# Two transformer blocks on one core: slots of the weight ring dealt by expected release, and two seams whose first weight tiles feed two units from four channel blocks

## What is computed

```
h = x + concat(mla(a), swa(a)) @ w_out            # a = rms_norm(x) ; a @ w_in feeds both attentions
h = h + square(relu(rms_norm(h) @ w_up)) @ w_down # first MLP, hidden width 8192
x = rms_norm(h)
mod = silu(c) @ w_ada + b_ada                     # 6 x 2048 values: shift, scale, gate (1 and 2)
z = (x * (1 + sc1) + sh1) @ w_in_2 + b_in_2       # 9216 wide: gating branch, hyena branch, gates
y_a = spatial_gating(...) @ w_branch_a ; y_b = hyena(...) @ w_branch_b
x = layer_norm(ALPHA * x + g1 * ((gate_a * y_a + gate_b * y_b) @ w_o + b_o))
h = x * (1 + sc2) + sh2
x = layer_norm(ALPHA * x + g2 * (square(relu(h @ w_m1 + b_m1)) @ w_m2 + b_m2))
```

## Time and profile before

| | |
|---|---|
| median of 3 runs | 2429.3 us (2428.83 to 2429.86) |
| profiled execution | 2428.58 us, of which the span in the trace is 2426.8 us |
| PE busy | 2376.5 us, 98% of the span |
| DVE, ACT busy | 1710.0 us (70%), 1049.4 us (43%) |
| loads of the stream | 498 of 1 MB, median 4.9 us from issue to landing |
| granted PE clock | 0.996 of full speed over the span |

### The profile page before, as it was taken

One profiled execution on the slowest core, in us unless ns is written; L12 is line 12 of the kernel. 1 busy time (PEld: TensorE's weight loads), 2 busy tenths in 40 slices (PEclk: granted clock), 3 DMA queues, 4 the chain that ended last, 5 costly groups with the idle time before them and its releaser, 6 DMA issues.

```text
span 2426.8 us, 30941 instructions
## 1 busy us (share of the span) xinstructions
PE 2376.5 (98%) x13376; PEld 2051.0 (85%) x13376; DVE 1710.0 (70%) x1559; ACT 1049.4 (43%) x999; POOL 29.8 (1%) x61
## 2 busy tenths in 40 slices
PE   7999999999999999989999999999999999999998
PEld 7998888888778888878888888997888888888887
DVE  7777577878777777765677666787764566774665
ACT  5464544434334334455645443343543443443443
POOL 0000000000000000000000000000000000000000
PEclk9999999999999999999999999999999999999999
DMA  7334477777777787775545547875455557775553
GB/s 274 134 130 151 174 262 287 288 290 271 280 294 278 296 309 285 299 268 189 211 162 181 184 177 269 299 278 200 173 190 197 186 190 301 273 278 211 186 193 110
DMA packets 79816, 558.73 MB, mean 230 GB/s; under 512 B 9034, under 2 KB 11285, under 8 KB 13248
## 3 DMA queue, kind: packets, MB, share of 16 engines
q1 hardware_dynamic: 74832, 528.25, 58.9%
q0 software_dynamic: 4848, 28.50, 3.3%
HBM read 547.26 MB, written 9.45 MB: 229 GB/s over the span
## 4 chain that ended last, share of the span: by engine, by line
PE 90%; DVE 4%; DMA 3%; ACT 2%; issue 1%; SPq 0%; ACTq 0%; DVEq 0%
PE ps L582 27%; PE ps L585 13%; PE ps L613 12%; PE ps L615 12%; PE ps L614 12%; DMA stage<-wstream 3%; PE ps L550 2%; PE ps L551 2%; PE ps L552 2%; DVE w_lo L1509 2%; ACT w_hi L1055 1%; PE ps L580 1%; PE ps L625 1%; PE ps L627 1%; PE ps L626 1%
## 5 line engine op out<-in xcount | busy, mean ns | idle before, releaser
L1509 DVE TENSOR_TENSOR w_lo<-stage,w_hi 128x2048 fp32r<-128x2048 f32 x402 | 918.4, 2288 | 459.0 <-ACT w_hi L1055 455.1
L1055 ACT ACTIVATE w_hi<-stage 128x2048 fp32r<-128x2048 f32 x402 | 766.6, 1911 | 755.1 <-DMA stage<-wstream 402.8
L582 PE MATMUL ps<-xs,w_hi 128*128 128x512 f32 x3200 | 998.5, 397 | 16.1 <-DVE w_lo L1509 14.0
L585 PEld LDWEIGHTS ps<-xs,w_lo 128*128 128x128 f32 x3000 | 564.9, 188 | 132.0
L585 PE MATMUL ps<-xs,w_lo 128*128 128x256 f32 x3000 | 591.6, 279 | 0.0
L582 PEld LDWEIGHTS ps<-xs,w_hi 128*128 128x128 f32 x3200 | 495.7, 189 | 31.2 <-DVE w_lo L1509 17.6
L613 PE MATMUL ps<-w_hi,hs 128*128 128x512 f32 x1008 | 394.4, 391 | 0.0
L615 PE MATMUL ps<-w_lo,hs 128*128 128x512 f32 x1008 | 392.7, 390 | 0.0
L614 PE MATMUL ps<-w_hi,hs 128*128 128x512 f32 x1008 | 392.6, 389 | 0.0
L613 PEld LDWEIGHTS ps<-w_hi,hs 128*128 128x128 f32 x1008 | 189.3, 188 | 41.7 <-issue 2.2
L614 PEld LDWEIGHTS ps<-w_hi,hs 128*128 128x128 f32 x1008 | 189.3, 188 | 39.7 <-issue 0.7
(11 more groups left out here) (414 smaller groups left out, 2248.2 us busy)
## 6 DMA issues: line engine op xcount, KB each, us to landing
stage<-wstream SPq DMA_DIRECT2D x497, 1024.0 KB, 4.9
spectra<-k_made POOLq DMA_DIRECT2D x4, 1024.0 KB, 7.7
k_spec<-spectra POOLq DMA_DIRECT2D x4, 1024.0 KB, 6.4
xraw<-xT SPq DMA_DIRECT2D x4, 512.0 KB, 11.4
resid<-x SPq DMA_DIRECT2D x2, 1024.0 KB, 15.7
w<-w POOLq DMA_DIRECT2D x16, 128.0 KB, 5.9
parked<-resid POOLq DMA_DIRECT2D x1, 2048.0 KB, 7.4
resid<-parked POOLq DMA_DIRECT2D x1, 2048.0 KB, 9.0
```

Source lines behind the costliest of these rows:

```text
L582: mm = pe.matmul(out[c], hi[c], rhs[:, k, :], start=(first and j == 0), stop=end)
L585: mm = pe.matmul(out[c][:, S:2 * S], lo[c], rhs[:, k, 0:S], start=False, stop=False)
L1055: act.activation(w_hi[:, w % HIGH, 0:m], stage[:, n % RING, 0:m], ACT.Copy).then_inc(hi_ready, 1)
L1509: tt(w_lo[:, slot, 0:m], stage[:, slot, 0:m], f(w_hi[:, w % HIGH, 0:m]), ALU.subtract).then_inc(lo_ready, 1)
```

## The change

**Slots.** `slots()` deals the five slots by an expected release time in units of tiles: a weight tile k frees its slot at k + 1.0, a chunk behind tile k at k - 1.1. Each load takes the slot that is expected free first and waits for what held it (`HELD_BY`). `ORDER` itself is as before, and so are `RING` and `HIGH`.

**Two-unit tiles.** Tiles 170 and 171 (and 274 and 275) are laid out anew ("quad"): each holds four of the 128-channel blocks (512 channels) of both units 80 and 81. Tile 170 needs block 0 alone, tile 171 block 1 alone. Tiles 172 and 173 hold the upper eight channel blocks of unit 80 and of unit 81, as before. The number of matmuls is the same.

**The seams' order.** PE turns two blocks before tile 170, block 2 in the middle of tile 170 and block 3 in the middle of tile 171. Of block 0 the first two of its four parts get a semaphore of their own (`first_turned`), so that DVE may begin after 4 of 8 transposes. ACT's scaling of block 3 stands behind its work on block 1. Tile 171 (275) is split at step 169 (273), which had no split; the waits of tile 171 for `seam_lower` and `seam_upper` are gone.

```diff
 WHERE = {what: n for n, what in enumerate(ORDER)}
+def slots():
+    free, uses = [-1.0 + i / RING for i in range(RING)], [0] * RING
+    held, k = [None] * RING, 0
+    slot, use, held_by = [], [], []
+    for n, (kind, i) in enumerate(ORDER):
+        k = i if kind == "w" else k
+        s = min(range(RING), key=lambda j: free[j])
+        uses[s] += 1
+        slot.append(s)
+        use.append(uses[s])
+        held_by.append(held[s])
+        held[s] = n
+        free[s] = k + 1.0 if kind == "w" else k - 1.1
+    return slot, use, held_by
+SLOT, USE, HELD_BY = slots()
 def place(w):
...
         return "tok", U_WOUT + n + (4 if kq >= 2 else 0), 4 * kq
+    if w in (T_Z, T_Z + 1):
+        return "quad", U_Z, 4 * (w - T_Z)
+    if w in (T_MLP2, T_MLP2 + 1):
+        return "quad", U_MLP2, 4 * (w - T_MLP2)
     if T_Z <= w < T_BA:
...
-    TURN = (4, 6, 2, 4)
+    TURN = (4, 6, 4, 6)
...
             m = columns_of(ORDER[n][1]) if ORDER[n][0] == "w" else TILE
-            sp.dma_start(stage[:, n % RING, 0:m], ws[n][:, 0:m]).then_inc(loaded[n % RING], 16)
+            sp.dma_start(stage[:, SLOT[n], 0:m], ws[n][:, 0:m]).then_inc(loaded[SLOT[n]], 16)
...
         load(4)
         for n in range(RING, len(ORDER)):
-            kind, k = ORDER[n - RING]
+            kind, k = ORDER[HELD_BY[n]]
             if kind == "w":
                 sp.wait_ge(tile_done, k + 1)
...
+        def two_units(w, rhs, k0, u, first, ready, hook):
+            for j in range(4):
+                k = k0 + j
+                if j == 2:
+                    hook()
+                if j % 2 == 0:
+                    pe.wait_ge(*ready(k // 2))
+                for v in range(2):
+                    out = [ps[:, 2 * ((u + v) % 2) + c, :] for c in range(2)]
+                    a = [1024 * v + (j * 2 + c) * P for c in range(2)]
+                    for c in range(2):
+                        pe.matmul(out[c], w_hi[:, w % HIGH, a[c]:a[c] + P], rhs[:, k, :], start=(first and j == 0),
+                                  stop=False)
+                    for c in range(2):
+                        mm = pe.matmul(out[c][:, S:2 * S], w_lo[:, SLOT[place(w)], a[c]:a[c] + P], rhs[:, k, 0:S],
+                                       start=False, stop=False)
+            return mm
         def tokens_apart(w, rhs, k0, u):
...
                 mm = weights_moved(w, rhs, 0, 4, u + 1, 1024, True, True, ready)
+            elif kind == "quad":
+                if first:
+                    pe.wait_ge(psum_free[(u + 1) % 2], (u + 1) // 2)
+                mm = two_units(w, rhs, k0, u, first, ready, hook)
             elif kind == "tok":
...
                 q, l = divmod(w - t0, QT)
                 if l < UPT:
-                    if t0 == T_MLP2 and w == t0 + 1:
-                        pe.wait_ge(sem("seam_lower"), since("ln1", "lower") + 3)
-                        pe.wait_ge(sem("seam_upper"), since("ln1", "upper") + 3)
-                    tile(w, xs, rhs_ready if w < t0 + 4 else None, hook if w == t0 else None)
+                    turn = (lambda: hook(2 + w - t0)) if hook is not None and w < t0 + 2 else None
+                    tile(w, xs, rhs_ready if w < t0 + 4 else None, turn)
                     if after is not None and w == t0:
                         after()
...
             elif n:
                 pe.wait_ge(sem("seam_scaled"), since(name, "scaled") + n)
-            if n == 3:
-                pe.wait_ge(sem("seam_lo"), since(name, "lo") + 2)
-            turn_block(n, TURN[n], (sem("seam_normed"), since(name, "normed")) if n == 0 else None).then_inc(sem("seam_turned"), 1)
+            if n >= 2:
+                pe.wait_ge(sem("seam_lo"), since(name, "lo") + n)
+            if n == 0:
+                for half in range(2):
+                    for t in range(NB):
+                        pe.wait_ge(sem("seam_normed"), since(name, "normed") + t + 1)
+                        for c in range(2):
+                            a = P * (2 * half + c)
+                            mm = pe.transpose(ps[:, TURN[0] + half, c * S + t * P:c * S + t * P + P],
+                                              resid[:, t, a:a + P], ident[:])
+                    mm.then_inc(sem("seam_turned" if half else "first_turned"), 1)
+                return
+            turn_block(n, TURN[n]).then_inc(sem("seam_turned"), 1)
...
-                pe.wait_ge(sem("seam_upper"), since("f", "upper") + 3)
             tile(w, xs, (lambda h: (sem("seam_lo"), since("f", "lo") + (h + 1 if h < 2 else h // 2 + 2))) if w < T_Z + 4 else None,
-                 (lambda: turn_normed("f", 3)) if w == T_Z else None)
+                 (lambda: turn_normed("f", 2 + w - T_Z)) if w < T_Z + 2 else None)
             if w in (T_Z + 10, T_Z + 14):
...
             turn_normed("ln1", n)
-        mlp(T_MLP2, U_MLP2, lambda h: (sem("seam_lo"), since("ln1", "lo") + (h + 1 if h < 2 else h // 2 + 2)), hook=lambda: turn_normed("ln1", 3))
+        mlp(T_MLP2, U_MLP2, lambda h: (sem("seam_lo"), since("ln1", "lo") + (h + 1 if h < 2 else h // 2 + 2)), hook=lambda n: turn_normed("ln1", n))
         pe.wait_ge(evac_done, U_END)
         for n in range(4):
             if n == 1:
...
             n = place(w)
-            act.wait_ge(loaded[n % RING], 16 * (n // RING + 1))
+            act.wait_ge(loaded[SLOT[n]], 16 * USE[n])
             if w >= HIGH:
                 act.wait_ge(tile_done, w - HIGH + 1)
             m = columns_of(w)
...
             act.activation(root_[:], var[:], ACT.Sqrt).then_inc(sem("token_root_ready"), 1)
-        def normed_hi(name, n, sh, sc, w):
+        def first_hi(name, sh, sc):
+            act.wait_ge(sem("seam_lower"), since(name, "lower") + 1)
+            act.activation(xs[:, 0:2, 0:S], turned[:, 0, 0:2], ACT.Copy).then_inc(sem("seam_hi"), 1)
+            act.wait_ge(sem("seam_turned"), since(name, "turned") + 1)
+            src = turned_bank(TURN[0])
+            for k in (2, 3):
+                ins = act.activation(turned[:, 0, k], src[:, k, :], ACT.Identity, bias=mod[:, sh + k:sh + k + 1],
+                                     scale=mod[:, sc + k:sc + k + 1])
+            ins.then_inc(sem("seam_upper"), 1)
+            act.wait_ge(sem("seam_upper"), since(name, "upper") + 1)
+            act.activation(xs[:, 2:4, 0:S], turned[:, 0, 2:4], ACT.Copy).then_inc(sem("seam_hi"), 1)
+        def normed_hi(name, n, sh, sc):
...
-                act.wait_ge(sem("seam_lower"), since(name, "lower") + 1)
-                act.activation(xs[:, 0:2, 0:S], turned[:, 0, 0:2], ACT.Copy).then_inc(sem("seam_hi"), 1)
-                act.wait_ge(sem("seam_upper"), since(name, "upper") + 1)
-                act.activation(xs[:, 2:4, 0:S], turned[:, 0, 2:4], ACT.Copy).then_inc(sem("seam_hi"), 1)
-                return
-            if n == 2:
-                split(w)
             act.wait_ge(sem("seam_upper"), since(name, "upper") + n + 1)
...
-        def into_stage(name, sh, sc, w):
+        def into_stage(name, sh, sc):
             act.wait_ge(sem("seam_scaled"), since(name, "scaled") + 1)
             scale_block(name, 2)
-            normed_hi(name, 0, sh, sc, w)
+            first_hi(name, sh, sc)
+            normed_hi(name, 1, sh, sc)
             scale_block(name, 3)
-            for n in range(1, 4):
-                normed_hi(name, n, sh, sc, w)
+            for n in range(2, 4):
+                normed_hi(name, n, sh, sc)
         act.wait_ge(sem("ones_ready"), 1)
...
-            if w not in LAST:
-                split(w + 2)
+            split(w + 2)
             if w == T_MLP1:
...
         for w in range(T_WO, T_MLP2):
-            if w not in LAST:
-                split(w + 2)
+            split(w + 2)
             if w == T_WO:
                 mix_hi(U_WO - 1)
...
-            dve.wait_ge(sem("seam_turned"), since(name, "turned") + n + 1)
+            if n:
+                dve.wait_ge(sem("seam_turned"), since(name, "turned") + n + 1)
+            else:
+                dve.wait_ge(sem("first_turned"), ("f", "ln1").index(name) + 1)
...
-        def into_stage(name, sh, sc, w):
+        def into_stage(name, sh, sc):
             normed(name, 0)
             normed(name, 1)
...
             normed_lower(name, 2, sh, sc)
-            split(w)
             normed_lo(name, 2)
...
         for w in range(T_WO, T_MLP2):
-            if w not in LAST:
-                split(w + 2)
-                condition(w + 2)
...
+def by_quarters(t):
+    both = [np.concatenate([t[0][:, a:a + TILE // 2], t[2][:, a:a + TILE // 2]], axis=1) for a in (0, TILE // 2)]
+    return np.concatenate([np.stack(both), t[[1, 3]], t[4:]])
```

More of the change, by code:

```diff
@@ L548, in weights_moved @@
                     o2 = acc(u)[:, c]
-                    hi, lo = w_hi[:, w % HIGH, a:a + P], w_lo[:, place(w) % RING, a:a + P]
+                    hi, lo = w_hi[:, w % HIGH, a:a + P], w_lo[:, SLOT[place(w)], a:a + P]
                     pe.matmul(o2, hi, rhs[:, k, 0:S], start=(first and j == 0), stop=False)
@@ L559, in narrow @@
```

(34 more changed lines are left out.)

9 lines of the change are left out of this document (2 added, 7 removed).

## The result

| | before | changed |
|---|---|---|
| median | 2429.4 us (4 runs, 2428.8 to 2429.9) | 2462.3 us (4 runs, 2460.8 to 2464.1) |
| profiled execution, its span | 2428.58, 2426.8 us | 2460.79, 2459.0 us |
| PE busy | 2376.5 us | 2388.2 us |

The ratio is 1.0136, with a 95% interval of 1.0118 to 1.0154: 33 us slower, where I had forecast 11 and a range that ended at 2449. The direction was right and the size was not.

A forecast was written before the change was run, and what follows sets the result against it. PE, busy 98% of the span, was taken as the bound. Loop 5.3, seams 0.6 and 2.0, clock 3.4 gave +11.3 us on 2428.58, 2439.9; the median 0.7 higher, 2440.6 us; range 2421 to 2449.

The forecast's parts named there:

- The loop: First MLP: load, high part, remainder, sum, next load take 11.28 us per two tiles, slower than PE; net +5.3 us.
- The start: Loop begins at tile 106's end, 702.09 us; the sum of a34 is ready 6.5 us later, at 708.6.
- The steps: From a34 to a69, 23 steps of 11.28 us and 12 of 7.1 us, 344.6 us in all.
- The credit: Second quarter of the first MLP: earlier loads remove its waits and give back 2.6 us.
- The bound above: Upper limit of the first MLP's term: +11 us, with hand-over delays at two pairs and loads 0.1 us longer.
- The load's duration: 1 MB load alone in the queue takes the row's 4.78 us, not the skill's estimated 4.4 us.
- Seam "f": Between tiles 169 and 172: first matmul 0.85 us earlier, but tile 172 starts +0.6 us late after a 3.6 us wait.
- Seam "ln1": Between tiles 273 and 276: tile 275's split delays the first token half 1.15 us; tile 276 starts +2.0 us late.
- The clock at the seams: Two new 3.6 us waits, each followed by 3.4 us at half clock: +3.4 us, bounds 0 and 6.8.
- Chunks a70 to a95: After seam "f": 11.28 us against PE's 11.17, 2.9 us behind at the end, less than the 5.6 us lead.
- A: Rival: slots work and the loop has room; first MLP gives 13 us, seams cost 2.6 to 6.0; chance 0.25.

The follow-up runs named there:

- k + 0.4: The changed kernel with a chunk's slot expected free at k + 0.4 in place of k - 1.1: 2423.4 us, ratio 0.9968.
- k - 0.6: The changed kernel with a chunk's slot expected free at k - 0.6 in place of k - 1.1: 2419.9 us, ratio 0.9954.
- The slots alone: The kernel before, its seams untouched, with the new table of slots: 2455.1 us, ratio 1.0096.
- the shorter sums: The changed kernel with DVE summing only 1024 or 1792 of each chunk's 2048 columns: 2420.8 us and 2444.9 us.
- the seams alone: The changed kernel with load n in slot n % 5 as before: 2439.3 us, ratio 1.0032.

## Why the prediction was right in direction and wrong in size

**The loop: right mechanism, its term mis-sized, 24.4 us and not 5.3.** The step that failed is this term: the loop's start, its count of slow steps and the 2.6 us given back. The forecast put the sum of a34 at 708.6 and that of a69 at 1053.2; the rest to the end of tile 169, 15.5 us, was right (15.7). Three parts make the 19 us:

- *The start, 5.8 us.* I let the loop begin at the end of tile 106, with everything ahead of it loaded, and put 6.5 us from there to the sum of a34. It was running already. The chain of waits of the changed kernel at that place:

```profile
695.91 4.85 DMA stage<-wstream
...
700.78 2.31 DVE stage L1875 x2
...
703.11 4.82 DMA stage<-wstream
...
707.95 1.93 ACT w_hi L1107
...
709.90 2.29 DVE w_lo L1565
712.19 2.22 DVE stage L1875 x2
...
714.42 6.95 DMA stage<-wstream
```

  The load of w109, which I had issued at 702.09 by tile 106's end, was held by the sum of a33 and issued at 703.11. That is only 1.0 us. The other 4.8 us are my 6.5: no row shows such a step, and from the issue of w109 to the sum of a34 it is a full turn of the loop, 11.3 us, as it was from w119's load on the earlier trace rows. The loop was in place long before: every load that waits for a chunk was issued within 0.03 us of that chunk's sum (in the kernel before 4 us or more behind it), and from a1 to a7 the steps are 11.3 to 11.4 us already. 17 chunks in 32 tiles are one in 1.9 tiles, nearly as dense as the third quarter's 19. The forecast said that they are rare there; its own count in the description of the stages said otherwise.
- *The steps, 10.5 us.* The 35 steps took 1069.5 - 714.4 = 355.1 us in place of 344.6. The ordinary step (11.3) and the short one (7.1 to 7.3) were right. But four of the twelve short ones took 8.34 us, and two of the others 12.91 and 13.45; these six are 8.8 of the 10.5 us. DVE in order of time shows one of the former, a43's sum (line 1875) at 806.27:

```profile
800.87 0.69 DVE L1890 SCALAR_TENSOR_TENSOR tev<-tev 128x512 f32<-128x512 f32 x1
802.26 0.69 DVE L1892 TENSOR_TENSOR hs<-tev,hs 128x512 fp32r<-128x512 f32 x1 [0.70 <-ACT hs L1348]
804.06 2.29 DVE L1565 TENSOR_TENSOR w_lo<-stage,w_hi 128x2048 fp32r<-128x2048 f32 x1 [1.11 <-ACT w_hi L1107]
806.27 2.28 DVE L1875 SCALAR_TENSOR_TENSOR stage<-stage,cond 128x2048 f32<-128x2048 f32 x1
```

  The unit's hand-over holds the next split on ACT, and the chunk's sum, which stands behind that split in DVE's order, starts only then; its load had landed at 805.14. The forecast had this as a bound, "about 1.3 us at a pair, two pairs"; it was 1.2 us at four. Of the long steps one is the same hand-over ahead of a56's sum. The other ends the chain above: w111's load took 6.95 us; the load before it in the queue, issued at 704.92, had not landed yet when it was issued, but at 717.84.
- *The credit, 2.6 us.* The end of the loop was a time on the clock, so the waits of the second quarter couldn't be taken off it once more. By the trace they didn't go either: 3.6 us of waits lie from 500 to 700 us.

**The bound above was too low.** I took +11 as the most the loop could cost. It had the hand-over at two pairs, not at four, no load behind a late one, and no case in which the loop is running already at a34, though nothing in the argument excluded it.

**The load's duration.** The loop's loads took 4.8 us from issue to landing, as the row of before had it. The Trainium skill, "DMA: Bandwidth & Descriptors", section "Anatomy of one DMA", would have it at 4.4 us by estimate, for POOL's path; these loads take another and were longer, and by that figure the loop would have been about as fast as PE.

**Seam "f": right.** Forecast +0.6, measured 0.6, with one wait of 3.58 us (forecast 3.6) in place of three. **Seam "ln1": right.** Forecast +2.0, measured 1.7; the idle time before the first transpose grew from 4.54 to 5.79, 1.25 for 1.15. **The clock at the seams: right, with some luck**, 3.4 us at half behind each. The wait before tile 172 left the clock alone at k + 0.4, and the one before tile 276 was followed by 6.8 us at half at k - 0.6 (last section). Running the split earlier shows that the wait hung on the order of ACT's and DVE's queues alone.

**Chunks a70 to a95: wrong.** I costed them at nothing. The stream is 3.7 us later between tiles 172 and 273; 1.7 us are the slow clock behind tile 172, which the forecast has in its term for the clock, and the other 2.0 us go with waits near 1557 and 1616 us, the largest of them for another result of DVE (who waited for whom, whole span, and DVE in order of time):

```profile
PE ps L668 <- DVE mixacc L2162: 1.5, 1, 1.5
```

```profile
1553.05 2.29 DVE L1565 TENSOR_TENSOR w_lo<-stage,w_hi 128x2048 fp32r<-128x2048 f32 x1 [3.00 <-ACT w_hi L1107]
1555.26 2.28 DVE L1875 SCALAR_TENSOR_TENSOR stage<-stage,cond 128x2048 f32<-128x2048 f32 x1
...
1557.46 0.68 DVE L2162 TENSOR_TENSOR mixacc<-mixacc,ps 128x512 f32<-128x512 f32 x1
```

The result stands behind a split and the sum of a72 on DVE, and that split's tile was loaded when a71 was summed: the loop again, by way of DVE's order. The slots alone have a shorter wait there (0.5 us); with the shorter sums, and with k - 0.6, there is none.

**Rivals.** A (the table helps, 2419 to 2422.5) was wrong for this table and right for its idea: with k - 0.6, 2419.9 us. Repeated gaps on the engine that should be full can mean too little room for the next tile, says the Trainium skill ("Perfetto Trace Analysis", section "Identifying Performance Opportunities"). The runs here show that five slots were enough: with k - 0.6 all of PE's waits for `w_lo` in the first MLP went with the same five.

## What to carry to other kernels

When buffers are dealt by an expected release time, follow for each buffer who frees it, and look for a way from release to release that doesn't pass through the engine that bounds the kernel. If that way is even 1% longer than this engine's own time for the same work, it takes over in the end. It is in place before the engine loses anything by it (here from a1 on, while nine tenths of the loss came behind tile 120): cost it over its whole length, with full turns, and with what else stands in the queues of its members. A table that expects a buffer's release a little later was 42 us faster here; and work that moves later on one engine (the fourth block) takes with it whatever is queued behind it there, so a split that PE needs soon goes ahead of it.

## What I had not expected of the hardware

Half clock lasted 3.4 us behind some waits and 6.8 behind others, of nearly the same length: 3.4 behind 4.14 us of idle PE, 6.8 behind 3.86 (both in the changed kernel's rows above). And the wait of 3.58 us before tile 172, which was followed by half clock in the changed kernel, was not in the run at k + 0.4, where the clock from 1074.6 to 1078.0 us is granted in full:

```profile
1074.56 0.73 PE L606 MATMUL ps<-xs,w_hi 128*128 128x512 f32 x2 [3.58 <-DVE w_lo L1565]
```

At k - 0.6 the wait of 3.57 us before tile 276 was followed by 6.8 us at half. A shorter idle stretch, of about 2.6 us, differs in the same way between two runs. At 551 us, the changed kernel after 2.56 us, and the slots alone after 2.57 us:

```profile
550.80:554.20 3.40, 3.40 (x19) 2.96 (x20) 3.40 (x3) 0.00 (x0) 0.00 (x0) 1.00 0.51 217
```

```profile
551.40:554.80 3.40, 3.40 (x10) 2.89 (x11) 3.40 (x3) 0.00 (x0) 0.00 (x0) 0.51 0.49 207
```

In the seams alone it came after only 1.89 us (908.3 to 911.7 us, granted 0.53), where 2.23 us of idle PE in the kernel before (ending at 904.61, in the stretch of the earlier trace rows) had left the clock alone. Waits of this length have a price that their length alone doesn't tell: one more reason to remove them rather than to shorten them.
